# The third and the last norm of a two-block transformer kernel: sums and roots on 128 columns, widened by four small products

## The chip, the cores and the metric

The kernel runs on one core of a Trainium2 chip. The metric is the device time of one execution in microseconds. The engines are TensorE (PE; its weight loads are listed as PEld), VectorE (DVE), ScalarE (ACT), GpSimd (POOL) and SyncE (SP), which issues the DMAs. Each has its own queue of instructions and works it off in order. They wait for each other by semaphores.

## The reference, cut to what matters

Two transformer layers follow each other on x with 512 tokens of 1024 features. Each has mixers and a feed-forward, and a norm over the features stands before each. The two norms that the change touches are the ones of the second layer:

```python
def _rms(x, w):
    xf = x.astype(jnp.float32)
    y = xf * lax.rsqrt(jnp.mean(xf * xf, axis=-1, keepdims=True) + EPS)
    return (y * w.astype(jnp.float32)).astype(x.dtype)

h = _rms(x, norm1_w[l]) * (1 + sc1) + sh1        # third norm, "r3": input of the second layer
proj = h @ w_in[l]
...
x = x + g1 * (mixed @ w_out[l])
h2 = _rms(x, norm2_w[l]) * (1 + sc2) + sh2       # last norm, "r6": input of its feed-forward
x = x + g2 * _conv_ffn(h2, w_up[l], conv_w[l], conv_b[l], w_down[l])
```

sc1, sh1, g1, sc2, sh2 and g2 come from a product of the conditioning vector c with w_mod (the "modulation").

## The kernel before, in words

**Layout.** x lies in SBUF as eight tiles of 128 features by 512 tokens (P = 128, KT = 8 tiles, S = 512 tokens, NT = 4 token blocks of 128). Weights come in chunks of 128x2048: SyncE loads a chunk (`load_chunk`, L113), ScalarE rounds it to its high part (`round_chunk`, L121), VectorE makes the low part (`rest_chunk`, L127), and TensorE multiplies in three passes, high by high, high by low, low by high (`split_mm`, L133 to L135). High and low parts have two slots each, so a chunk is rounded while the one before it is multiplied.

**A norm** (class `Norm`, L167 to L207). ScalarE squares the eight tiles (L179), GpSimd adds the first of them into `acc` (L188), and TensorE adds over the features: a product of a 128x128 matrix of ones with `acc` (L194) and with each square tile that was not added (L197). The result is the sum of each token, the same in all 128 rows of a bank, for 512 tokens. ScalarE takes the root of mean plus EPS (L202), 128x512, and VectorE the reciprocal (L207), 128x512, into `root`, which other products on VectorE then use as a full tile. An fp32 product appears in the trace as two records.

**Third norm, r3.** It stands at the end of the block with the first layer's feed-forward. GpSimd adds six squares, TensorE adds the sum and the last square tile (`r3.pe_sum(pe, k, KT - 2, [KT - 1])`), and then makes six modulation reductions (L447), each of three products with one column, 36 records together. ScalarE's order at the end of this block is: last square, root, rounding of the second weight chunk of the next block. VectorE's is: last addition to x, reciprocal, low part of that chunk. Then the semaphores of the block are cleared and all engines meet at a barrier. The next block begins with eight tiles scaled by VectorE (`shifted_dve`: L227 scales, L235 makes the low part) and rounded by ScalarE (`shifted_act`, L242); TensorE multiplies each as it comes.

**Last norm, r6.** It stands between the output projection of the second layer and its feed-forward, in one block. GpSimd adds four squares, and TensorE adds their sum and four square tiles (`r6.pe_sum(pe, k, KT - 5, list(range(KT - 4, KT)))`). ScalarE's order there is: rounding of a feed-forward chunk, squares 6 and 7, root, then the eight roundings of `shifted_act`. VectorE's is: last additions to x (L2415), low part of that chunk (`rest_chunk(dve, k, (OUT2 + 5) % 2, OUT2 + 6)`), reciprocal, wait for it, `shifted_dve`. TensorE goes on with the first feed-forward chunk, tile by tile as the scaled tiles are split (`ffn2.pe_up(pe, i, h6_split if i == 0 else None)`). The two first chunks of the feed-forward are loaded, rounded and split before the reciprocal.

**Small products that the kernel already has.** `group_sums` (L646) and the lag weights (L2152) write 32 rows of a bank each, with 32 columns of weights; `group_spread` (L651) and the state inputs (L2128) read 32 rows each.

**Order.** Nothing is planned by a program: the order on each engine is the order in which its code is written out.

Of the kernel before, what the change touches and what calls it, by code (L numbers as in the profile page):

```python
# [9 lines left out]
ACT = mybir.ActivationFunctionType  # L10
# [3 lines left out]
P = 128  # L14
S = 512
D = 1024
KT = D // P
NT = S // P
# [7 lines left out]
EPS = 1e-6  # L26
# [140 lines left out]
class Norm:  # L167
# [37 lines left out]
    def dve_invert(self, dve):  # L205
        dve.wait_ge(self.rooted, 1)
        dve.reciprocal(self.root[:, :], self.root[:, :]).then_inc(self.inverted, 1)  # L207

# [388 lines left out]
def program(nc, io):  # L597
    root_ctx = ExitStack()
    with root_ctx:
        k = Core()  # L600
# [9 lines left out]
        def sb(name, shape, dt=F, ctx=root_ctx):  # L610
            return ctx.enter_context(nc.sbuf_tensor(name, shape, dt))
# [12 lines left out]
        eps_col = sb("eps_col", [P, 1])  # L624
        sqrt_first = sb("sqrt_first", [P, 2])
# [43 lines left out]
        def gone(ctx):  # L669
            ctx.close()  # L670
# [135 lines left out]
        with nc.Block() as block:  # L806
# [20 lines left out]
            @block.gpsimd  # L827
            def _(pool):
                pool.memset(k.ones[:, :], 1.0).then_inc(set_up, 1)
                pool.memset(eps_col[:, :], EPS).then_inc(set_up, 1)  # L830
                pool.memset(neg_ones[:, :], -1.0).then_inc(set_up, 1)
                pool.memset(windows[:, :, :, NCMP:32], 0.0).then_inc(set_up, 1)
                pool.memset(spread[:, :], 0.0).then_inc(set_up, 1)
# [580 lines left out]
        r2, r3 = Norm(k, "r2", square_sum, k.root, k.bank[6]), Norm(k, "r3", square_sum, k.root, k.bank[6])  # L1414
# [15 lines left out]
        with nc.Block() as block:  # L1430
# [82 lines left out]
            def _(act):  # L1513
# [44 lines left out]
                r3.act_root(act, KT, eps_col[:, 0:1])  # L1558
# [3 lines left out]
            def _(dve):  # L1562
# [49 lines left out]
                r3.dve_invert(dve)  # L1612
                ffn.dve_weights(dve, ffn.down_chunk(1, KT - 1) + 2)

            @block.tensor
            def _(pe):
# [40 lines left out]
                for c in range(modulation.AT_END, modulation.N):  # L1657
                    modulation.reduce(pe, c)
        gone(ffn_ctx)
# [648 lines left out]
        r6 = Norm(k, "r6", square_sum, k.root, k.bank[6])  # L2308
# [8 lines left out]
        with nc.Block() as block:  # L2317
# [31 lines left out]
            def _(act):  # L2349
# [34 lines left out]
                r6.act_root(act, KT, eps_col[:, 0:1])  # L2384
# [8 lines left out]
            def _(dve):  # L2393
# [52 lines left out]
                dve.wait_ge(r6.inverted, 1)  # L2446
# [10 lines left out]
            def _(pe):  # L2457
# [41 lines left out]
                r6.pe_sum(pe, k, KT - 5, list(range(KT - 4, KT)))  # L2499
                for half in range(2):  # L2500
                    for i in range(HALF * half, HALF * half + HALF):
                        ffn2.pe_up(pe, i, h6_split if i == 0 else None)
                    for j in range(KT):
                        ffn2.pe_down(pe, half, j)
# [146 lines left out]
```

## Time and profile before

| | us |
|---|---|
| median of 3 runs | 1347.76 (1345.07 to 1348.29) |
| profiled execution, its own time | 1347.27 |
| span of the profiled execution | 1345.5 |
| TensorE busy | 1261.2 (94%) |
| VectorE busy | 783.7 (58%) |
| ScalarE busy | 505.3 (38%) |
| GpSimd busy | 130.1 (10%) |
| mean granted clock of TensorE | 0.968 of 2.4 GHz |

The profiled execution's own time is 1.8 us longer than its span. A row of a timeline has the start and the length in us from the span's start, the engine, the line of the kernel, the operation, what is written from what, shapes and count, and in brackets how long the engine had been idle before and what ended that. A row of a group has the count, busy time in us and mean length of one in ns. TensorE's clock is given as a share: 1.00 is 2.4 GHz, 0.50 is 1.2 GHz.

### The profile page before, as it was taken

Reading aid. Unit: us, or ns where it says so; the run is one execution under the profiler, and the core shown is the slowest. Engines: PE = TensorE matmul, PEld = TensorE weight load, DVE = VectorE, ACT = ScalarE, POOL = GpSimd, SP = SyncE. Lnnn points to the kernel's source line nnn. Section 1 sums busy time; section 2 is a strip of 40 time slices with the busy share of each in tenths; the row PEclk is TensorE's granted clock in tenths of the full one; section 3 lists DMA queues with packets and bytes.
Section 4 is the critical chain, followed back from the end, with each engine's and each line's share of the span. In section 5 each row is a group of like instructions: output and inputs, shape, how many; then the busy total and the mean of one; then the engine's idle time right before and its main releaser. Section 6 shows DMA issues by size and latency. Waiting matters only on the chain. (4 is left out here: it accounts for less than half of the span.)

```text
span 1345.5 us, 15518 instructions
## 1 busy us (share of the span) xinstructions
PE 1261.2 (94%) x6278; PEld 985.3 (73%) x6278; DVE 783.7 (58%) x1254; ACT 505.3 (38%) x768; POOL 130.1 (10%) x124
## 2 busy tenths in 40 slices
PE   6999998779999999999999899769899999999999
PEld 5786675437788878888887686447678878888877
DVE  5656674234475695566554785866865553366532
ACT  5244445744432211222222722455344331233321
POOL 0000000001400170000011560003400000000000
PEclk9999999888999999999999879899989999999999
DMA  9311113010244445444443341010303222322222
GB/s 366 101 42 63 63 32 113 13 63 32 94 165 164 145 132 198 166 165 164 135 160 112 98 75 58 1 64 32 125 32 97 101 77 90 121 94 94 84 98 84
DMA packets 24678, 138.42 MB, mean 103 GB/s; under 512 B 2623, under 2 KB 4896, under 8 KB 15264
## 3 DMA queue, kind: packets, MB, share of 16 engines
q1 hardware_dynamic: 24608, 137.43, 30.4%
q8 instruction: 50, 0.82, 0.2%
q14 instruction: 20, 0.16, 0.0%
HBM read 133.75 MB, written 3.67 MB: 102 GB/s over the span
## 5 line engine op out<-in xcount | busy, mean ns | idle before, releaser
L133 PE MATMUL bank<-xhi_ffn,w_hi_part 128*128 128x512 f32 x704 | 278.7, 396 | 6.6 <-DVE xlo_ffn L235 6.6
L134 PE MATMUL bank<-xlo_ffn,w_hi_part 128*128 128x512 f32 x704 | 277.7, 394 | 0.0
L135 PE MATMUL bank<-xhi_ffn,w_lo_part 128*128 128x512 f32 x704 | 275.9, 392 | 0.0
L121 ACT ACTIVATE w_hi_part<-w_raw 128x2048 fp32r<-128x2048 f32 (+1 forms) x96 | 165.7, 1726 | 275.4 <-PE bank L135 270.4
L127 DVE TENSOR_TENSOR w_lo_part<-w_raw,w_hi_part 128x2048 fp32r<-128x2048 f32 (+1 forms) x96 | 198.8, 2071 | 88.9 <-ACT w_hi_part L121 85.6
L133 PEld LDWEIGHTS bank<-xhi_ffn,w_hi_part 128*128 128x128 f32 x704 | 133.3, 189 | 36.6 <-issue 7.6
L135 PEld LDWEIGHTS bank<-xhi_ffn,w_lo_part 128*128 128x128 f32 x704 | 133.2, 189 | 29.6
L134 PEld LDWEIGHTS bank<-xlo_ffn,w_hi_part 128*128 128x128 f32 x704 | 132.9, 189 | 27.9 <-issue 0.2
L362 DVE SCALAR_TENSOR_TENSOR squares<-bank,param,squares 128x511 f32<-128x511 f32 x88 | 63.9, 747 | 86.0 <-ACT squares L345 84.4
L134 PE MATMUL bank<-hlo_half,w_hi_part 128*128 128x512 f32 x240 | 96.6, 402 | 0.0
L133 PE MATMUL bank<-hhi_half,w_hi_part 128*128 128x512 f32 x240 | 96.0, 400 | 0.5 <-DVE hlo_half L334 0.5
L133 PE MATMUL bank<-hhi,w_hi_part 128*128 128x512 f32 x240 | 94.6, 394 | 1.7 <-DVE hlo L370 1.7
L135 PE MATMUL bank<-hhi_half,w_lo_part 128*128 128x512 f32 x240 | 95.3, 397 | 0.0
L134 PE MATMUL bank<-hlo,w_hi_part 128*128 128x512 f32 x240 | 93.6, 390 | 0.0
L135 PE MATMUL bank<-hhi,w_lo_part 128*128 128x512 f32 x240 | 93.5, 390 | 0.0
L437 DVE SCALAR_TENSOR_TENSOR mod_acc<-mod_w,mod_c,mod_acc 128x384 f32<-128x384 f32 x112 | 75.7, 676 | 2.6
L133 PE MATMUL bank<-xhi,w_hi_part 128*128 128x512 f32 x144 | 61.2, 425 | 11.5 <-DVE w_lo_part L937 11.5
L345 ACT ACTIVATE squares<-bank,param 128x512 f32<-128x512 f32 x44 | 31.9, 776 | 84.1 <-PE bank L135 84.1
L135 PE MATMUL bank<-xhi,w_lo_part 128*128 128x512 f32 x144 | 57.1, 397 | 0.0
L322 DVE TENSOR_TENSOR squares<-bank,rms_root 128x512 f32<-128x512 f32 x22 | 15.2, 691 | 71.6 <-PE bank L135 71.5
L134 PE MATMUL bank<-xlo,w_hi_part 128*128 128x512 f32 x144 | 56.8, 394 | 0.0
L133 PEld LDWEIGHTS bank<-hhi_half,w_hi_part 128*128 128x128 f32 x240 | 45.7, 190 | 13.9 <-issue 1.5
(365 smaller groups left out, 2024.6 us busy)
## 6 DMA issues: line engine op xcount, KB each, us to landing
mod_w<-in_w_mod SPq DMA_DIRECT2D x32, 768.0 KB, 4.4
w_raw<-in_w_gu SPq DMA_DIRECT2D x22, 1024.0 KB, 4.8
w_raw<-in_w_down SPq DMA_DIRECT2D x32, 704.0 KB, 4.1
w_raw<-in_w_up SPq DMA_DIRECT2D x22, 1024.0 KB, 4.7
w_raw<-in_w_in_f SPq DMA_DIRECT2D x9, 1024.0 KB, 5.1
w_raw<-in_w_out SPq DMA_DIRECT2D x8, 1024.0 KB, 4.8
w_raw<-in_w_in SPq DMA_DIRECT2D x5, 1024.0 KB, 4.9
x<-in_x SPq DMA_DIRECT2D x4, 512.0 KB, 8.6
```

What stands on the lines that cost most here:

```text
L121: act.activation(k.whi[:, slot, 0:width], k.raw[:, slot, 0:width], ACT.Copy).then_inc(k.w_hi, 1)
L127: dve.tensor_tensor(k.wlo[:, slot, 0:width], k.raw[:, slot, 0:width], k.whi[:, slot, 0:width].bitcast(F), ALU.subtract).then_inc(k.w_lo, 1)
L133: pe.matmul(out, whi, xhi, start=first, stop=False)
L134: pe.matmul(out, whi, xlo, start=False, stop=False)
L135: return pe.matmul(out, wlo, xhi, start=False, stop=last)
L322: dve.tensor_tensor(gate, k.bank[a][:, :], root, ALU.mult).then_inc(self.gated, 1)
L345: act.activation(k.sq[:, s, :], k.bank[s][:, :], ACT.Identity, bias=bias[:, 2 * i + a:2 * i + a + 1], scale=taps[:, 6 * i + 3 * a + 2:6 * ...
L362: dve.scalar_tensor_tensor(out=y, in0=k.bank[s][:, 0:S - back], scalar=taps[:, tap:tap + 1], in1=y, op0=ALU.mult, op1=ALU.add).then_inc(se ...
L437: ins = dve.scalar_tensor_tensor(out=acc, in0=w, scalar=self.c[:, j:j + 1], in1=acc, op0=ALU.mult, op1=ALU.add)
```

## The change

The third and the last norm become a `QuarterNorm`. Its sum makes, of each tile, four products of 128 columns (one block of tokens each) with 32 columns of ones; the product of token block q is written to rows 32q to 32q + 31 of one bank, all in columns 0 to 127. Root and reciprocal then work on 128x128. The root is taken of 1024 times mean plus EPS (a second constant column, filled by GpSimd at the start), so it is 32 times as large. Four products with 32 rows each then add 32 equal rows of the reciprocal into all 128 rows, each in the columns of its token block and in a bank of its own (banks 2 to 5). ScalarE copies two of the four results into `root`, VectorE the other two. At r3 the widening stands behind the second of the six reductions on TensorE, and the copies stand before the rounding and the low part of the next chunk; at r6 VectorE waits for all four copies before it scales.

```diff
@@ -205,6 +205,54 @@
     def dve_invert(self, dve):
         dve.wait_ge(self.rooted, 1)
         dve.reciprocal(self.root[:, :], self.root[:, :]).then_inc(self.inverted, 1)
+
+
+class QuarterNorm(Norm):
+
+
+    def __init__(self, k, name, acc, root, bank, wide):
+        super().__init__(k, name, acc, root, bank)
+        self.wide, self.small = wide, acc[:, 0:P]
+        self.widened, self.copied = k.sem(f"{name}_widened"), k.sem(f"{name}_copied")
+
+    def pe_sum(self, pe, k, added, tail):
+        pe.wait_ge(self.added, added)
+        for n, j in enumerate([None] + list(tail)):
+            if j is not None:
+                pe.wait_ge(self.squared, j + 1)
+            src = self.acc if j is None else k.sq[:, j % 4, :]
+            for q in range(NT):
+                mm = pe.matmul(self.bank[32 * q:32 * q + 32, 0:P], k.ones[:, 0:32], src[:, P * q:P * q + P],
+                               start=(n == 0), stop=(n == len(tail)))
+        mm.then_inc(self.summed, 1)
+
+    def act_root(self, act, n, eps_col):
+        act.wait_ge(self.summed, 1)
+        act.activation(self.small, self.bank[:, 0:P], ACT.Sqrt, bias=eps_col, scale=1024.0 / (P * n))\
+            .then_inc(self.rooted, 1)
+
+    def dve_invert(self, dve):
+        dve.wait_ge(self.rooted, 1)
+        dve.reciprocal(self.small, self.small).then_inc(self.inverted, 1)
+
+    def pe_widen(self, pe, k):
+        pe.wait_ge(self.inverted, 1)
+        for q in range(NT):
+            pe.matmul(self.wide[q][:, P * q:P * q + P], k.ones[32 * q:32 * q + 32, :],
+                      self.small[32 * q:32 * q + 32, :], start=True, stop=True).then_inc(self.widened, 1)
+
+    def copy(self, q):
+        return self.root[:, P * q:P * q + P], self.wide[q][:, P * q:P * q + P]
+
+    def act_copy(self, act):
+        for q in (0, 1):
+            act.wait_ge(self.widened, q + 1)
+            act.activation(*self.copy(q), ACT.Copy).then_inc(self.copied, 1)
+
+    def dve_copy(self, dve):
+        for q in (2, 3):
+            dve.wait_ge(self.widened, q + 1)
+            dve.tensor_copy(*self.copy(q)).then_inc(self.copied, 1)
 
 
 def plain_round(act, norm, hi, src, gain):
@@ -622,6 +670,7 @@
         spread = sb("spread", [P, 2 * P])
         k.ones = sb("ones", [P, P])
         eps_col = sb("eps_col", [P, 1])
+        eps_wide = sb("eps_wide", [P, 1])
         sqrt_first = sb("sqrt_first", [P, 2])
         mods = sb("mods", [P, 48])
 
@@ -827,6 +876,7 @@
             @block.gpsimd
             def _(pool):
                 pool.memset(k.ones[:, :], 1.0).then_inc(set_up, 1)
+                pool.memset(eps_wide[:, :], 1024.0 * EPS)
                 pool.memset(eps_col[:, :], EPS).then_inc(set_up, 1)
                 pool.memset(neg_ones[:, :], -1.0).then_inc(set_up, 1)
                 pool.memset(windows[:, :, :, NCMP:32], 0.0).then_inc(set_up, 1)
@@ -1411,7 +1461,8 @@
         hlo = sb("hlo_half", [P, HALF, S], R, ffn_ctx)
         ghi, glo = hhi[:, 0:KT, :], hlo[:, 0:KT, :]
         modulation = Modulation(k, io, sb, ffn_ctx, pr, mods, keep_sem)
-        r2, r3 = Norm(k, "r2", square_sum, k.root, k.bank[6]), Norm(k, "r3", square_sum, k.root, k.bank[6])
+        r2 = Norm(k, "r2", square_sum, k.root, k.bank[6])
+        r3 = QuarterNorm(k, "r3", square_sum, k.root, k.bank[6], k.bank[2:6])
         ffn = FeedForward(k, "ffn", GU, io["w_gu"], io["w_down"], xhi, xlo, hhi, hlo, following=2)
         gn_sq, gn_sq_v, gn_took, gn_root, gn_inv, gn_wide, gn_scaled, gn_hi, gn_lo, added1 = (
             k.sem(f"group_{w}") for w in ("squared", "squared_v", "taken", "rooted", "inverted", "spread", "scaled",
@@ -1555,7 +1606,8 @@
                             r3.act_square(act, k, x[:, j, :], j)
                         if half == 0 or j < KT - 1:
                             ffn.act_weights(act, ffn.down_chunk(half, j) + 2)
-                r3.act_root(act, KT, eps_col[:, 0:1])
+                r3.act_root(act, KT, eps_wide[:, 0:1])
+                r3.act_copy(act)
                 ffn.act_weights(act, ffn.down_chunk(1, KT - 1) + 2)
 
             @block.vector
@@ -1610,6 +1662,7 @@
                             dve.scalar_tensor_tensor(out=scale1, in0=scale1, scalar=1.0, in1=pr("norm1"), op0=ALU.add,
                                                      op1=ALU.mult)
                 r3.dve_invert(dve)
+                r3.dve_copy(dve)
                 ffn.dve_weights(dve, ffn.down_chunk(1, KT - 1) + 2)
 
             @block.tensor
@@ -1656,6 +1709,8 @@
                 r3.pe_sum(pe, k, KT - 2, [KT - 1])
                 for c in range(modulation.AT_END, modulation.N):
                     modulation.reduce(pe, c)
+                    if c == modulation.AT_END + 1:
+                        r3.pe_widen(pe, k)
         gone(ffn_ctx)
 
 
@@ -2305,7 +2360,7 @@
         sum_b = sb("square_sum_ssm", [P, S], ctx=tail_ctx)
         r5 = Norm(k, "r5", square_sum, root_a, k.bank[6])
         r4 = Norm(k, "r4", sum_b, root_b, k.bank[7])
-        r6 = Norm(k, "r6", square_sum, k.root, k.bank[6])
+        r6 = QuarterNorm(k, "r6", square_sum, k.root, k.bank[6], k.bank[2:6])
         h6_scaled, h6_rounded, h6_split = k.sem("norm2_scaled"), k.sem("norm2_rounded"), k.sem("norm2_split")
         out_a, part_a, part_b, added_a, added_b, stored = (
             k.sem(f"out2_{w}") for w in ("attn", "attn_scaled", "ssm_scaled", "attn_added", "added",
@@ -2381,7 +2436,8 @@
                         r6.act_square(act, k, x[:, j, :], j)
                     if c == 3:
                         round_chunk(act, k, n % 2, 16 * (n // 2 + 1), n - 1)
-                r6.act_root(act, KT, eps_col[:, 0:1])
+                r6.act_root(act, KT, eps_wide[:, 0:1])
+                r6.act_copy(act)
                 shifted_act(act, k, h6_scaled, h6_rounded, lambda j: shift2[:, j:j + 1], xhi)
                 for half in range(2):
                     for i in range(HALF * half, HALF * half + HALF):
@@ -2443,7 +2499,8 @@
                 from_ssm(3)
                 rest_chunk(dve, k, (OUT2 + 5) % 2, OUT2 + 6)
                 r6.dve_invert(dve)
-                dve.wait_ge(r6.inverted, 1)
+                r6.dve_copy(dve)
+                dve.wait_ge(r6.copied, 4)
                 shifted_dve(dve, k, h6_scaled, h6_rounded, h6_split, x, lambda j: scale2[:, j:j + 1],
                             lambda j: shift2[:, j:j + 1], xhi, xlo)
                 for half in range(2):
@@ -2497,6 +2554,7 @@
                 out2(3, bank_b[3], 0, k.w_used)
                 pe.wait_ge(part_a, 6)
                 r6.pe_sum(pe, k, KT - 5, list(range(KT - 4, KT)))
+                r6.pe_widen(pe, k)
                 for half in range(2):
                     for i in range(HALF * half, HALF * half + HALF):
                         ffn2.pe_up(pe, i, h6_split if i == 0 else None)
```

## Rows read from the trace of the kernel before

**Rows 1.** The page, part 1: busy time, share of the span, records of TensorE.
```profile
PE 1261.2 (94%) x6278; PEld 985.3 (73%) x6278; DVE 783.7 (58%) x1254; ACT 505.3 (38%) x768; POOL 130.1 (10%) x124
```

**Rows 2.** Timeline around r3: start, length, engine, line, operation, idle before.
```profile
732.56 1.13 PE L197 MATMUL bank<-squares,ones 128*128 128x512 f32 x2 [0.58 <-ACT squares L179]
733.52 4.07 PE L447 MATMUL bank<-ones,mod_acc 128*128 128x1 f32 x36
733.72 0.69 ACT L202 ACTIVATE rms_root<-bank,eps_col 128x512 f32<-128x512 f32 x1 [1.22 <-PE bank L197]
734.31 1.90 ACT L121 ACTIVATE w_hi_part<-w_raw 128x2048 fp32r<-128x2048 f32 x1
734.44 3.35 DVE L207 RECIPROCAL rms_root<-rms_root 128x512 f32<-128x512 f32 x1 [2.60 <-ACT rms_root L202]
737.71 2.23 DVE L127 TENSOR_TENSOR w_lo_part<-w_raw,w_hi_part 128x2048 fp32r<-128x2048 f32 x1
742.06 1.42 DVE L227 SCALAR_TENSOR_TENSOR squares<-x,mods,rms_root 128x512 f32<-128x512 f32 x2 [2.12 <-PEq L1663]
...
744.50 0.77 PE L133 MATMUL bank<-xhi_in,w_hi_part 128*128 128x512 f32 x1 [6.91 <-DVE xlo_in L235]
```

**Rows 3.** Timeline around r6.
```profile
968.44 1.23 ACT L179 ACTIVATE squares<-x 128x512 f32<-128x512 f32 x2
968.92 2.29 DVE L127 TENSOR_TENSOR w_lo_part<-w_raw,w_hi_part 128x2048 fp32r<-128x2048 f32 x1
...
969.12 1.98 PE L197 MATMUL bank<-squares,ones 128*128 128x512 f32 x4 [0.19 <-ACT squares L179]
...
971.14 0.69 ACT L202 ACTIVATE rms_root<-bank,eps_col 128x512 f32<-128x512 f32 x1 [1.47 <-PE bank L197]
971.86 3.35 DVE L207 RECIPROCAL rms_root<-rms_root 128x512 f32<-128x512 f32 x1 [0.66 <-ACT rms_root L202]
975.25 1.41 DVE L227 SCALAR_TENSOR_TENSOR squares<-x,mods,rms_root 128x512 f32<-128x512 f32 x2
...
977.69 0.77 PE L133 MATMUL bank<-xhi_ffn,w_hi_part 128*128 128x512 f32 x1 [6.58 <-DVE xlo_ffn L235]
```

**Rows 4.** Timelines of small products: 32 rows written (L2152), 32 rows read (L651).
```profile
834.92 2.02 PE L2152 MATMUL bank<-c_lifted,b_turned 128*32 128x128 f32 x64
...
82.68 1.14 PE L651 MATMUL bank<-head_roots,spread 32*128 32x512 f32 x8
...
298.19 2.09 PE L651 MATMUL bank<-square_sum,spread 32*128 32x512 f32 x8 [4.16 <-DVE square_sum L1568]
```

**Rows 5.** Groups by line and shape, small operations of VectorE and ScalarE.
```profile
L1054 DVE RECIPROCAL sq_cmp<-sq_cmp 128x31 f32<-128x31 f32 x1 | 0.3, 342 | 0.0
L1384 DVE SCALAR_TENSOR_TENSOR keep<-bank,soft 128x128 f32<-128x128 f32 x4 | 1.1, 284 | 0.0
...
L900 ACT ACTIVATE sq_cmp<-bank,eps_col 128x31 f32<-128x31 f32 x1 | 0.3, 286 | 2.1 <-PE bank L1244 2.1
L1358 ACT ACTIVATE attn<-bank 128x128 f32<-128x128 f32 x4 | 1.1, 282 | 0.1
```

**Rows 6.** Stretches: length, TensorE busy (records), granted clock, DMA share, GB/s.
```profile
297.80:297.90 0.10, 0.00 (x0) 0.50 0.00 0
...
738.10:738.20 0.10, 0.00 (x0) 0.50 0.00 0
748.30:748.40 0.10, 0.10 (x1) 0.80 0.00 0
...
973.60:973.70 0.10, 0.00 (x0) 0.60 1.16 492
...
983.80:983.90 0.10, 0.10 (x2) 0.70 0.00 0
```

**Rows 7.** Timeline of the first microseconds.
```profile
0.87 0.10 POOL L830 MEMSET eps_col<- 128x1 f32 x1
...
5.72 1.28 ACT L212 ACT_TABLE_LOAD   x1 [5.72 <-DMA x<-in_x]
```

## The prediction

> **What bounds the kernel now.** I read the page first: TensorE is busy for 94% of the span [rows 1], so only the stretches in which it waits, or runs at its lower clock, have anything to give. Then I read the timeline of the two norms that the change touches. In both the reader should follow one chain: the last square on ScalarE, its sum on TensorE, the root on ScalarE, the reciprocal on VectorE, and what follows the reciprocal. Last I read the granted clock around both.
>
> At r6 the chain is bare. The last pair of squares ends at 969.67 (968.44 + 1.23), the last sums end at 971.10, the root runs 971.14 to 971.83, the reciprocal 971.86 to 975.21, the first scaled tile starts at 975.25, and TensorE begins the feed-forward at 977.69 after 6.58 us without a product [rows 3]. Behind that nothing but TensorE decides, so what is cut here reaches the end of the kernel.
>
> At r3 it is not bare. The reciprocal ends at 737.79, but VectorE then makes the low part of the next weight chunk (737.71 to 739.94), then comes the end of the block, and the next stage's first scaled tile is at 742.06 [rows 2]. That low part needs the high part, which ScalarE makes from 734.31 to 736.21, directly after the root. So there the reciprocal's place is the last thing but one, and ScalarE's queue stands close behind it.
>
> The clock: it falls to half (1.2 GHz) at 973.6, inside r6's gap, and returns to 2.4 GHz at 983.8, which is 6.1 us after the first product; in r3's gap it falls at 738.1 and is back at 748.3, 3.8 us after the first product at 744.50 [rows 2, 3, 6].
>
> **The change, part by part.**
>
> *Sums.* One full product (two records of 512 columns) becomes four products of 128 columns with 32 columns of weights, eight records, each product in its own 32 rows of the bank. The nearest row is 64 records of 128 columns with 128*32 weights, in all four row blocks of a bank: 2.02 us together, 0.03 us each, where a stream of them in line would need four times that [rows 4]. So the four run beside each other. A last tile cost 1.13 us before (732.56 to 733.69) [rows 2]; now I take 0.5 us: two passes, their spread and the run-out. The other bound is no overlap, about 1.1 us, as before.
>
> The Trainium skill has a rule that speaks against this: "TensorE: Matmul & The Clock Gate", section "The mechanism", says that a weight load overlaps a running product only if the row group differs, and here all 128 rows are used each time. By that rule the eight records of a tile would stand in line and cost as much as now. The row of 64 records disagrees with it, and I go by the row.
>
> *What that is worth at r6.* Without the change the root ends at 971.83. With it the sums end near 970.2 and the root near 970.6. But VectorE is busy until 971.21 with the low part of a weight chunk [rows 3], and the reciprocal stands behind it in VectorE's order. So it starts at 971.24 instead of 971.86: 0.6 us won, not 1.6, and even sums in line would cost only 0.2 of that. This is what is late next.
>
> *Root.* 0.69 us for 512 columns [rows 3], 286 ns for 31 [rows 5]; in proportion 0.37 us for 128.
>
> *Reciprocal.* 3.35 us for 512 columns [rows 3], 0.34 us for 31 [rows 5]: 6.26 ns a column, so 0.95 us for 128. It saves 2.40 us at either place. At r6 it ends at 972.19.
>
> *Widening, new.* Four products of 32 rows, eight records, into four banks. Eight such records with 512 columns take 1.14 us at full clock and 2.09 us at half clock [rows 4, 6]. For 128 columns I take 0.1 us to start and 0.8 us (bounds 0.5, for a quarter of the columns with the run-out kept, and 1.1, the same eight records at full clock with all 512 columns). Before, the clock fell 2.5 us after the last sum [rows 3, 6]; the widening now comes 2.1 us after it, so it may meet the lower clock, and this is why I don't take the lower bound. At r6 the fourth product ends at 973.1.
>
> *Copies, new.* ScalarE and VectorE take two each. Copies of 128x128 from a bank are 282 ns on ScalarE, and an operation of VectorE on 128x128 from a bank is 284 ns [rows 5]. Two in a row, the first begun while the last products run, and the wait for all four: 0.6 us after the last product (bounds 0.4 and 0.9). Scaling would start at 973.7; I take 973.75 against 975.25.
>
> So at r6: 0.6 + 2.4 - 0.9 - 0.6 = **1.5 us earlier** (bounds 0.9 and 2.0). The first product of the feed-forward moves from 977.69 to 976.2.
>
> *Clock at r6.* During the first 6.1 us TensorE ran at half, which cost 3.1 us [rows 3, 6]. The gap that remains (970.2 to 976.2, with only the widening in it) is still long, so the clock will still fall. When it comes back is not tied to the first product alone: 6.1 us here, 3.8 us at r3. I take the middle, 5.0 us, which gives back (6.1 - 5.0)/2 = 0.6 us. Bounds: a return at the same moment as now costs half of the shift (0.75 us lost); a return after 3.8 us gives 1.2 us.
>
> *r3.* Sum 0.6 earlier (nothing is in VectorE's way there), root to 733.45, reciprocal to 734.45. But the widening stands behind two of the six reductions in TensorE's order: 36 records take 4.07 us [rows 2], 12 take 1.4, to about 734.4, so it runs 734.6 to 735.4. ScalarE's two copies end near 735.8. The rounding of the next chunk (1.90 us) stands behind them: it ends at 737.7 where it ended at 736.21. VectorE's low part (2.23 us), which waited for nothing but the reciprocal, now waits for that rounding and starts at 737.75 instead of 737.71. So 2.4 us of reciprocal buy nothing: **0.1 us later** with the wait between engines. TensorE's remaining 24 reductions end near 738.1 at full clock and near 740.8 if the clock is already down (twice 0.113 each), which is 0.9 us behind the low part and would be the upper bound. The lower bound is 0.3 us earlier. SyncE's first transfers of the next block move with its start, by the same 0.1 us; the weights of its first products are rounded in this block.
>
> *Small parts.* Six more products in r3's sums and fifteen in r6's cost nothing: the sums of the earlier tiles stand before a wait for squares (TensorE waits 0.58 us for the last one at r3 and 0.19 us at r6 [rows 2, 3]); without that cover they would be in the 1.1 us bound of a tile. Changing between full array, column blocks and row blocks: the Trainium skill ("TensorEngine Tiling (Array Packing)", "Key Properties") says that a change of mode drains the array. It gives no figure; no term of the sum takes one from it. The new constant is one more fill on GpSimd in the first microsecond (such a fill takes 0.10 us), while ScalarE waits for x until 5.72 [rows 7]: nothing, or 0.1 us without that cover. No weight transfer is issued later at r6, since SyncE waits for low parts that are made before the reciprocal. Two more semaphores to clear at the block's end: under 0.1 us.
>
> **Sum.** +0.1 - 1.5 - 0.6 = -2.0 us. Against the profiled execution, 1347.27 us (span 1345.5), that is 1345.3. The median of the three runs shown is 0.5 higher, so I forecast 1345.8 for the median. 0.3%, about 4.0 us, is what a measurement of this kernel can tell from no change; the forecast is inside it.
>
> **Rivals.**
> *The clock helps more.* The work left in the gap, or the moment at which it begins, spares the half-clock stretch of r6: 3.1 us instead of 0.6, so 1345.8 - 2.5 = 1343.3. For it: the gap shrinks and the widening stands in it. Against: at r3 the clock fell with reductions running nearly to that moment [rows 2, 6], so small products did not hold it there. Chance 0.14. In its better half, with 0.5 us more at the widening and a fast r3, it passes -4.
> *The clock takes back.* It returns at the same moment as now, or later for r3: +0.75 instead of -0.6, giving 1347.1. For it: 3.8 and 6.1 us differ without a reason in the work. Chance 0.22.
> *The change doesn't do what it says.* The small products stand in line, and widening plus copies take 2.5 us: r6 gains 3.0 - 0.2 - 2.5 = 0.3 us, giving 1347.5 with no clock gain. Against: rows 4. Chance 0.07.
> *Slower, through ScalarE's place at r3.* ScalarE waits for the widening with the next chunk's rounding queued behind it, and TensorE reaches the widening late and on a low clock. The block ends 0.9 us later by the bound above; the next stage's first product at 744.50 then comes after 745, and if the clock's return moves from 3.8 us behind it to r6's 6.1, another 1.2 us go. With r6's lower bound (0.9) and its clock at the same moment (+0.75): 0.9 + 1.2 - 0.9 + 0.75 = +1.95, or 1349.7. It decides once the block's end moves by more than r6 gains, 1.5 us. Chance 0.09.
> The forecast itself keeps 0.48.
>
> **How the numbers follow.** The forecast's own range is 1344.5 to 1347.0. The range given, 1342.9 to 1348.3, takes in the first three rivals with the 1.5 us or so by which runs of one kernel lie apart, and leaves out the slow end and the best of the clock. Faster by over 0.3% (under 1343.7) needs the first rival or a lucky median: 0.16. Slower by over 0.3% (over 1351.8) needs more than the slower rival gives: 0.04. Within: 0.80.
>
> **What would show it.** Right: last sum records at r6 ending near 970.2 relative to squares at 969.67; a reciprocal of about 0.95 us that starts when the low part ends; scaling 2.5 us after the low part's end (before 4.0); a gap before the first product of about 5 us; at r3 the rounding after two small copies and the low part waiting for ScalarE, the next stage at 742 +/- 0.5. Wrong: column-block products at 0.1 us each, copies over 0.4 us, TensorE's reductions as the last work of r3's block, or a clock that never falls in r6's gap.

## The result, and the profile after

| | before | after |
|---|---|---|
| median of six runs, us | 1345.55 (1342.59 to 1348.29) | 1358.09 (1355.93 to 1361.02) |
| profiled execution, its own time, us | 1347.27 | 1361.0 |
| its span, us | 1345.5 | 1359.1 |
| mean granted clock | 0.968 | 0.962 |

The ratio is 1.0113, with an interval of 1.0093 to 1.0133: the changed kernel is 1.1% slower (0.9% by the medians), where the prediction had it the same, at 1345.8 us. The ratios here and below are estimated from the single runs and differ from the quotient of the medians by up to 0.2%. Two executions further on, one of the kernel before (4341 us) and one of e2_noshift (5534 us), took several times as long as all others and are in no median and no ratio.

The page of after answers to [rows 1]; the second line is a group of its part 5 (line, operation, count, then busy us and mean ns of one, then idle time before it and what ended that):

```profile
PE 1279.8 (94%) x6336; PEld 989.8 (73%) x6336; DVE 779.7 (57%) x1258; ACT 506.2 (37%) x772; POOL 130.2 (10%) x125
...
L133 PE MATMUL bank<-xhi_ffn,w_hi_part 128*128 128x512 f32 x704 | 279.2, 397 | 3.1 <-DVE xlo_ffn L283 3.1
```

TensorE is busy 18.6 us longer (1279.8 for 1261.2), with only 58 records of small products added (6336 for 6278). The wait ahead of the feed-forward's first product is 3.1 us instead of 6.6, but the widening now stands in the gap and splits it: from the end of the last sum to that product it is 5.6 us (976.97 to 982.60) for 6.6 before. So the last norm's own chain is shorter, and the loss has to be looked for elsewhere.

**The last norm of after**, the timeline that answers to [rows 3]:

```profile
975.26 1.23 ACT L179 ACTIVATE squares<-x 128x512 f32<-128x512 f32 x2
975.75 2.28 DVE L127 TENSOR_TENSOR w_lo_part<-w_raw,w_hi_part 128x2048 fp32r<-128x2048 f32 x1
975.94 0.43 PE L225 MATMUL bank<-squares,ones 128*32 128x128 f32 x8 [1.97 <-ACT squares L179]
976.54 0.43 PE L225 MATMUL bank<-squares,ones 128*32 128x128 f32 x8 [0.17 <-ACT squares L179]
977.04 0.37 ACT L231 ACTIVATE square_sum<-bank,eps_wide 128x128 f32<-128x128 f32 x1 [0.55 <-PE bank L225]
977.95 0.94 DVE L236 RECIPROCAL square_sum<-square_sum 128x128 f32<-128x128 f32 x1
978.95 0.61 PE L241 MATMUL bank<-square_sum,ones 32*128 32x128 f32 x8 [1.97 <-DVE square_sum L236]
979.55 0.45 ACT L250 ACTIVATE rms_root<-bank 128x128 f32<-128x128 f32 x2 [2.15 <-PE bank L241]
979.64 0.49 DVE L255 COPY rms_root<-bank 128x128 f32<-128x128 f32 x2 [0.75 <-PE bank L241]
980.16 1.41 DVE L275 SCALAR_TENSOR_TENSOR squares<-x,mods,rms_root 128x512 f32<-128x512 f32 x2
...
982.60 0.77 PE L133 MATMUL bank<-xhi_ffn,w_hi_part 128*128 128x512 f32 x1 [3.05 <-DVE xlo_ffn L283]
```

From the start of the last squares to the scaling it is 4.90 us (975.26 to 980.16), where it was 6.81 (968.44 to 975.25), so 1.9 us less.

**The third norm of after**, which answers to [rows 2]:

```profile
736.29 0.63 ACT L179 ACTIVATE squares<-x 128x512 f32<-128x512 f32 x1 [5.23 <-DVE x L425]
736.97 0.42 PE L225 MATMUL bank<-squares,ones 128*32 128x128 f32 x8 [1.08 <-ACT squares L179]
737.33 1.50 PE L495 MATMUL bank<-ones,mod_acc 128*128 128x1 f32 x12
737.47 0.37 ACT L231 ACTIVATE square_sum<-bank,eps_wide 128x128 f32<-128x128 f32 x1 [0.55 <-PE bank L225]
737.87 0.95 DVE L236 RECIPROCAL square_sum<-square_sum 128x128 f32<-128x128 f32 x1 [1.61 <-ACT square_sum L231]
738.88 0.50 PE L241 MATMUL bank<-square_sum,ones 32*128 32x128 f32 x8
...
739.73 1.91 ACT L121 ACTIVATE w_hi_part<-w_raw 128x2048 fp32r<-128x2048 f32 x1
741.67 2.29 DVE L127 TENSOR_TENSOR w_lo_part<-w_raw,w_hi_part 128x2048 fp32r<-128x2048 f32 x1 [1.70 <-ACT w_hi_part L121]
```

The next stage's first scaling comes at 746.10, 9.81 us after the start of the last square; before it was 10.18 (731.88 to 742.06).

**Where the time went.** I compared the starts of ScalarE's weight roundings (L121), which mark every chunk of products, in both profiled executions. After is 2.1 us behind by 60 us and still at 223, 5.0 at 322 (the clock fell at other moments in between), 5.4 at the third norm, 6.8 at 966 us, and only 3.8 at 993 us, at the first rounding behind the last norm. From there it loses a little with every chunk, up to 13.2 at the last rounding. Of the last feed-forward, two roundings next to each other for each of its two sizes of chunk, before:

```profile
1036.66 1.91 ACT L121 ACTIVATE w_hi_part<-w_raw 128x2048 fp32r<-128x2048 f32 x1
1047.54 1.91 ACT L121 ACTIVATE w_hi_part<-w_raw 128x2048 fp32r<-128x2048 f32 x1
...
1124.23 1.38 ACT L121 ACTIVATE w_hi_part<-w_raw 128x1408 fp32r<-128x1408 f32 x1 [6.10 <-PE bank L135]
1131.71 1.38 ACT L121 ACTIVATE w_hi_part<-w_raw 128x1408 fp32r<-128x1408 f32 x1 [6.10 <-PE bank L135]
```

and after:

```profile
1041.78 1.91 ACT L121 ACTIVATE w_hi_part<-w_raw 128x2048 fp32r<-128x2048 f32 x1
1052.98 1.91 ACT L121 ACTIVATE w_hi_part<-w_raw 128x2048 fp32r<-128x2048 f32 x1
...
1124.00 1.38 ACT L121 ACTIVATE w_hi_part<-w_raw 128x1408 fp32r<-128x1408 f32 x1 [6.32 <-PE bank L135]
1131.71 1.38 ACT L121 ACTIVATE w_hi_part<-w_raw 128x1408 fp32r<-128x1408 f32 x1 [6.32 <-PE bank L135]
```

A chunk of 48 products takes 11.20 us in place of 10.88, one of 33 takes 7.70 or 7.71 in place of 7.48. With 22 and 16 such chunks that is 22 x 0.32 + 16 x 0.22 = 10.6 us, most of the 12.5 between the medians. The clock is not it. TensorE in the stretch from 1000 to 1300 us (length, TensorE busy and its products, granted clock, DMA share, GB/s), before:

```profile
1000.00:1300.00 300.00, 298.31 (x1315) 1.00 0.28 94
```

and after:

```profile
1000.00:1300.00 300.00, 299.34 (x1284) 1.00 0.27 90
```

Both run at 2.4 GHz throughout and TensorE hardly pauses, yet 31 products fewer fit in: 298.31/1315 = 226.9 ns from product to product before, 299.34/1284 = 233.1 after. No instruction of this stage was changed.

What was changed is where its tiles lie. `eps_wide`, the second constant column, is an SBUF tile of its own, and the addresses of the built program show what it does: everything that is laid down behind it is 32 bytes further on. The weight tiles stand in front and stay (`w_hi_part` at 49280, which is 128 modulo 256); in the last feed-forward the high and low input tiles that are streamed through them go from 88192 and 116864 (128 modulo 256, both) to 88224 and 116896, the hidden high and low tiles from 133248 and 155776 (128 both) to 133280 and 155808. I call the distance of a streamed tile from the weight tile, modulo 256, its relative place: 0 before, 32 after, in the whole last feed-forward. The first feed-forward had its high input tile at 0 and its low and hidden tiles at 96; now they are at 32 and 128. Its chunks of 48 products took 11.10 us before and take 11.10 after (435.00 to 446.10 before, 439.88 to 450.98 after), its chunks of 33 took 7.70 and take 7.67.

### The profile page after: what moved, and what is told of

The parts are those of the page before. It is cut to its first block and busy times, and to the rows that moved or that the text cites. A ratio compares the mean times of both kernels' runs of the same rounds, so it can differ in the third digit from the quotient of the medians.

```text
span 1359.1 us, 15643 instructions
## 1 busy us (share of the span) xinstructions
PE 1279.8 (94%) x6336; PEld 989.8 (73%) x6336; DVE 779.7 (57%) x1258; ACT 506.2 (37%) x772; POOL 130.2 (10%) x125
## 5 line engine op out<-in xcount | busy, mean ns | idle before, releaser
L133 PE MATMUL bank<-xhi_ffn,w_hi_part 128*128 128x512 f32 x704 | 279.2, 397 | 3.1 <-DVE xlo_ffn L283 3.1
L134 PE MATMUL bank<-xlo_ffn,w_hi_part 128*128 128x512 f32 x704 | 278.3, 395 | 0.0
L135 PE MATMUL bank<-xhi_ffn,w_lo_part 128*128 128x512 f32 x704 | 277.7, 394 | 0.0
L121 ACT ACTIVATE w_hi_part<-w_raw 128x2048 fp32r<-128x2048 f32 (+1 forms) x96 | 165.7, 1726 | 280.8 <-PE bank L135 277.1
L133 PEld LDWEIGHTS bank<-xhi_ffn,w_hi_part 128*128 128x128 f32 x704 | 132.4, 188 | 35.1 <-issue 3.6
L135 PEld LDWEIGHTS bank<-xhi_ffn,w_lo_part 128*128 128x128 f32 x704 | 132.5, 188 | 31.4
L134 PEld LDWEIGHTS bank<-xlo_ffn,w_hi_part 128*128 128x128 f32 x704 | 132.6, 188 | 31.2 <-issue 0.2
L133 PE MATMUL bank<-hhi,w_hi_part 128*128 128x512 f32 x240 | 95.8, 399 | 1.3 <-DVE hlo L418 1.3
L133 PE MATMUL bank<-hhi_half,w_hi_part 128*128 128x512 f32 x240 | 96.3, 401 | 0.5 <-DVE hlo_half L382 0.5
L134 PE MATMUL bank<-hlo_half,w_hi_part 128*128 128x512 f32 x240 | 95.8, 399 | 0.0
L135 PE MATMUL bank<-hhi_half,w_lo_part 128*128 128x512 f32 x240 | 95.6, 398 | 0.0
L134 PE MATMUL bank<-hlo,w_hi_part 128*128 128x512 f32 x240 | 94.8, 395 | 0.0
L135 PE MATMUL bank<-hhi,w_lo_part 128*128 128x512 f32 x240 | 94.8, 395 | 0.0
L133 PE MATMUL bank<-xhi,w_hi_part 128*128 128x512 f32 x144 | 61.9, 430 | 11.6 <-DVE w_lo_part L987 11.6
L134 PE MATMUL bank<-xlo,w_hi_part 128*128 128x512 f32 x144 | 57.7, 401 | 0.0
L135 PE MATMUL bank<-xhi,w_lo_part 128*128 128x512 f32 x144 | 57.6, 400 | 0.0
L133 PEld LDWEIGHTS bank<-hhi_half,w_hi_part 128*128 128x128 f32 x240 | 45.9, 191 | 13.2 <-issue 1.5
```

Of the source, the lines that this page charges most:

```text
L121: act.activation(k.whi[:, slot, 0:width], k.raw[:, slot, 0:width], ACT.Copy).then_inc(k.w_hi, 1)
L133: pe.matmul(out, whi, xhi, start=first, stop=False)
L134: pe.matmul(out, whi, xlo, start=False, stop=False)
L135: return pe.matmul(out, wlo, xhi, start=False, stop=last)
```

## The experiments

Theory P (place): the 32 bytes are the loss, since the spacing of the products hangs on the relative place (theory A in the texts written before the runs). Rivals: the new instructions or waits of the norms, or the phase of the clock behind them. Ratios are against the kernel before on the same chip. In the cuts of code, "..." stands for lines that only follow from those shown.

**The shift without the change, and the change without the shift**

```diff
 # e1_pad: the kernel before, with
+        unused = sb("unused", [P, 1])          # between eps_col and sqrt_first
 # e2_noshift: the changed kernel, with
-        eps_col = sb("eps_col", [P, 1])
-        eps_wide = sb("eps_wide", [P, 1])
+        eps_col = sb("eps_col", [P, 2])
+        eps_wide = eps_col[:, 1:2]
...
 # e3_shift64: the changed kernel, with
+        unused = sb("unused", [P, 1])          # behind eps_wide: 64 bytes in all
```

> The kernel before with one unused tile of 32 bytes a partition between eps_col and sqrt_first; no instruction is added, and the norms are the old ones. Theory A (the place in SBUF: the new constant column pushes every later tile up by 32 bytes, and products that read them are some 7 ns apart further): 1359 us or so, 12 to 15 above the kernel before, and feed-forward chunks of the second layer 11.20 us apart instead of 10.88. Theory B (small products leave TensorE slower behind them): no change, 1346, 10.88 us. Theory C (longer or differently placed instruction streams): no change either, 1346.

> The changed kernel with the second constant in a second column of eps_col, so that no tile moves. Theory A: second feed-forward chunks 10.88 us apart as before, and the gain of the last norm alone is left: 1343 to 1345, 1 to 4 under the kernel before. Theory B: slow chunks (11.20 us) from the last norm on, 1354 or more. Theory C: as the changed kernel, 1358.

> The changed kernel with one more unused tile of 32 bytes, so that the later tiles are up by 64 bytes. Theory A in the form that a start at a multiple of 64 bytes counts: 10.88 us chunks again, 1343 to 1345. Theory A in the form that only one certain place is good: 11.2 us chunks, 1358. Theories B and C: 1358.

| | median, us | before | ratio | us per chunk of 48 |
|---|---|---|---|---|
| e1_pad | 1359.34 (4 runs) | 1347.51 (28 runs) | 1.0092 [1.0070, 1.0114] | 11.20 |
| e2_noshift | 1348.14 (11) | 1347.51 | 1.0013 [0.9996, 1.0030] | 10.88 |
| e3_shift64 | 1351.29 (10) | 1347.51 | 1.0029 [1.0014, 1.0044] | 10.99 |

An unused tile of 32 bytes in the old kernel costs what the whole change costs. The stretch of e1_pad that answers to the two above:

```profile
1000.00:1300.00 300.00, 298.70 (x1279) 1.00 0.26 89
```

and that of e2_noshift, with the new norms and no shift:

```profile
1000.00:1300.00 300.00, 298.31 (x1315) 1.00 0.27 93
```

e2 has the 1315 products of before. P stands, and the norms are ruled out as the cause of the loss. e2's time is a miss all the same: I had expected 1343 to 1345, and it isn't faster than before. e3 fell between its two forecasts (1343 to 1345, or 1358): it is not simply further from the old place, the worse, since 64 bytes cost a third of what 32 do.

**One norm at a time**, both with `eps_wide` in the second column of `eps_col`:

```diff
 # e4_r6_noshift: third norm as before
-        r3 = QuarterNorm(k, "r3", square_sum, k.root, k.bank[6], k.bank[2:6])
+        r3 = Norm(k, "r3", square_sum, k.root, k.bank[6])
...
 # e5_r3_noshift: the same for the last norm, r6
...
```

> No tile moves, the last norm is the new one, the third norm is the old one. Theory A and my step for the third norm (worth nothing, 0.1 us later): as e2_noshift within 1 us, 1343 to 1345. If the third norm's change costs time through ScalarE's queue, this is faster than e2_noshift by what it costs.

> No tile moves, the third norm is the new one, the last norm the old one. From the traces (last square to the next stage's first scaled tile took 10.18 us with the old third norm and 9.80 with the new one in e2_noshift): 0.4 us faster than the kernel before, that is no difference that can be measured. If the third norm's change is what keeps e2_noshift 1.9 us over e4_r6_noshift, 1.5 to 2 us slower than the kernel before.

e4: 1346.67 (12 runs, before 1347.51), 0.9987 [0.9974, 1.0000]. e5: 1348.79 (12 runs, before 1348.30), 1.0010 [0.9997, 1.0023]. I had expected e4 at 1343 to 1345 too. The last norm alone is 0.13% faster (1.8 us by the ratio, 0.8 by the medians), with an interval that reaches down to no change; the third alone gains nothing. In e4's trace the last squares start at 966.52 and the scaling at 971.65, 5.13 us: 1.7 of the 1.9 us again, as in all four others with the new last norm (e2, e3, e8, e10: 5.12 or 5.13). The rest is the widening, which in e4 ran at half clock and took 0.81 us:

```profile
970.21 0.81 PE L241 MATMUL bank<-square_sum,ones 32*128 32x128 f32 x8 [1.98 <-DVE square_sum L236]
```

**Absolute or relative, and which tiles**

```diff
 # e6_allshift: the kernel before, all tiles from x on, weights too, 32 bytes on
+        unused = sb("unused", [P, 8])
 # e11_weights32: the same 32 bytes ahead of the weight tiles alone, and 224 behind them
+        unused = sb("unused", [P, 8])
...
+        unused_b = sb("unused_b", [P, 56])
 # e9_tail32: the kernel before, last feed-forward's low and hidden tiles 32 bytes on
+        unused_tail = sb("unused_tail", [P, 8], ctx=tail_ctx)
 # e10_after256: the changed kernel, everything behind eps_wide 256 bytes on
+        unused = sb("unused", [P, 56])
```

> The kernel before with an unused tile of 32 bytes in front of x, so that all tiles move up by 32 bytes, the weight tiles as well as the tiles that TensorE streams. If the place of the streamed tile by itself counts (absolute): as e1_pad, chunks of the second feed-forward 11.20 us apart, 1356 to 1360. If its place relative to the weights counts: 10.88 us, 1346.

> The kernel before with the two weight tiles up by 32 bytes and all tiles behind them up by 256. Relative theory: the streamed tiles are now 32 bytes behind the weights' place, chunks of the second feed-forward near 11.2 us and the time 10 us or more over the kernel before, though no streamed tile moved against 256. Absolute theory: as before, 10.88 us.

> The kernel before with an unused tile of 32 bytes in front of xlo_ffn2 only: xhi of the second feed-forward, and everything before it, stays; xlo_ffn2, hhi2 and hlo2 go up by 32 bytes. If the place counts product by product: the down chunks (33 products, both tiles moved) go from 7.48 to 7.70 us, the up chunks (48 products, one third of them reading the moved tile) from 10.88 to about 10.98, 22 x 0.1 + 16 x 0.22 = 5.7 us over the kernel before. If one badly placed tile slows everything: 10 to 11 us over it. If something in the constant or in an earlier stage is to blame: no change.

> The changed kernel, its constant tile included, with 224 more unused bytes, so that the later tiles are up by 256 bytes. Place theory with a period of 256 bytes: as e2_noshift, chunks of 10.88 us, 1346 to 1349, within 0.3% of the kernel before. If any shift costs: 1358.

| | relative place in the last feed-forward | products, 1000 to 1300 us | ns each | ratio |
|---|---|---|---|---|
| e6_allshift | 0 (absolute: all +32) | 1315 | 226.9 | 0.9964 [0.9947, 0.9980] |
| e11_weights32 | 224 (weights +32) | 1280 | 233.4 | 1.0076 [1.0053, 1.0099] |
| e9_tail32 | high 0, low and hidden 32 | 1289 | 231.7 | 1.0064 [1.0042, 1.0086] |
| e10_after256 | 0 (streamed tiles +256) | 1315 | 226.9 | 1.0010 [0.9993, 1.0028] |

The medians are 1344.43 (7 runs, before 1348.30), and 1359.10 (4), 1356.91 (4) and 1348.57 us (10) with 1347.83 before. e6 moves every tile and keeps the spacing, e11 leaves the streamed tiles at the same place modulo 256 and moves the weights, and pays in full. So it is the relative place, and e10 says that a whole 256 bytes are as good as none. The stretches of e6, e11 and e10:

```profile
1000.00:1300.00 300.00, 298.30 (x1315) 1.00 0.27 93
...
1000.00:1300.00 300.00, 298.71 (x1280) 1.00 0.27 92
...
1000.00:1300.00 300.00, 298.30 (x1315) 1.00 0.27 92
```

The chunks of 33 products are the cleanest measure, since both tiles that they stream, the hidden high and low, lie at one relative place. Over both feed-forwards and all runs they take 7.48 us at 0 (before, last feed-forward; e7, first), 7.70 at 32 (after, e1, e9), 7.55 at 64 (e3, last; e11, first), 7.70 at 96 (before, first), 7.67 at 128 (after, first), 7.73 at 160 (e3, first) and 7.70 at 224 (e11, last). Place 64 gives the same in either feed-forward, whichever of the tiles was moved to get there, and half of 256 is no good place.

e6 is 0.36% faster than before, with the same instructions and the same spacing. Its profile differs from before in where the clock falls (1.3 us up to 322, 0.8 at 920, 1.6 at the last norm); why that should come with all tiles moved I can't say. So two builds can lie 0.3% apart outside the interval of their runs, and differences of 0.1 to 0.3% (e2, e4, e5, e10) are no safer than that. The 0.6 to 0.9% of e1, e7, e9 and e11 are, and their chunk times show where they arise.

e9 missed. I expected 5.7 us over before in all and measured 0.64%, 8.6 us. With only the low tile moved in the up products (the chunks of 48), I expected a third of 0.32 us a chunk and measured 0.21 (1039.08, 1050.17, 1061.27: 11.09). The products of one such chunk show why:

```profile
1039.62 0.39 PE L133 MATMUL bank<-xhi_ffn,w_hi_part 128*128 128x512 f32 x1
1039.85 0.40 PE L134 MATMUL bank<-xlo_ffn,w_hi_part 128*128 128x512 f32 x1
1040.09 0.39 PE L135 MATMUL bank<-xhi_ffn,w_lo_part 128*128 128x512 f32 x1
1040.31 0.39 PE L133 MATMUL bank<-xhi_ffn,w_hi_part 128*128 128x512 f32 x1
1040.55 0.40 PE L134 MATMUL bank<-xlo_ffn,w_hi_part 128*128 128x512 f32 x1
1040.78 0.39 PE L135 MATMUL bank<-xhi_ffn,w_lo_part 128*128 128x512 f32 x1
```

From L133 to L134 and from L134 to L135 it is 0.23 to 0.24 us each, and only from L135 back to L133 is it 0.22: three products take 0.69 in place of 0.68, since the step into the low tile's product and the step out of it are both long. One product in three with a moved tile costs two thirds of the price (0.21 of 0.32). The prices of the tiles don't simply add, either: with the high tile at 32 and the low one at 128 (after, first feed-forward) a chunk of 48 takes 11.10 us, less than the 11.20 with both at 32. No run shows the rule for two tiles at different places.

**The other way round: the first feed-forward, placed well.** If P holds, its tiles at 96 leave time lying there.

```diff
 # e7_ffn1_place: the kernel before, low and hidden tiles of the first feed-forward to place 0
+        unused_ffn = sb("unused_ffn", [P, 40], ctx=ffn_ctx)
 # e8_r6_placed: e4 with that line, and the second mixer's low input tile to place 0
+        unused_in2 = sb("unused_in2", [P, 32], ctx=mix_ctx)
```

> The kernel before with an unused tile of 160 bytes in front of the tiles of the first feed-forward, so that xlo_ffn1, hhi_half and hlo_half start at the same place modulo 256 as the tiles of the second (they are 96 bytes behind it now, and products there are 231 to 234 ns apart instead of 227). The place theory: 22 chunks of 48 products faster by 0.2 us, 16 of 33 by 0.2 and 4 of 48 by 0.3, 8 to 9 us together, 1338. Anything else that differs between the two feed-forwards (VectorE's modulation products, their weight traffic): 1346, chunks 11.1 us apart as now.

> The new last norm alone, no shift from the constant, the first feed-forward placed as in e7_ffn1_place, and the low input tile of the second layer's input projection moved by 128 bytes. The place theory: e7's gain plus the 1.2 to 2 us of e4_r6_noshift, 1336 to 1337. Else 1345.

e7: 1338.46 (4 runs, before 1348.30), 0.9918 [0.9898, 0.9939]. The gain is 9.8 us by the medians, for 8 to 9 expected; by the roundings, e7 gets 8.4 us ahead between 322 us and the third norm (12.9 for 4.5), and so does e8. The rest is the clock's moments. Its chunks of 48 in the first feed-forward take 10.88 us (428.12 to 439.00) for 11.10. TensorE in the middle of that stage (small reductions are among the products), before:

```profile
420.00:680.00 260.00, 259.53 (x1152) 1.00 0.47 158
```

and in e7, with 17 more in the same time:

```profile
420.00:680.00 260.00, 258.98 (x1169) 1.00 0.48 160
```

e8: 1337.94 (5 runs, before 1348.30), 0.9920 [0.9907, 0.9933]. It beats both kernels, but stands level with e7 and a microsecond above what was expected of it (1336 to 1337): beside the placement, the new last norm shows nothing that can be told apart.

## Why the prediction was wrong

**The step that failed** is among the small parts: "The new constant is one more fill on GpSimd in the first microsecond [...]: nothing, or 0.1 us without that cover." The fill does cost nothing. The tile it fills costs 0.92% by e1, about 12.4 us (11.8 by the medians), because it moves every tile behind it. I had counted the instruction and not its storage, and had taken it that unchanged products keep their spacing. None of the rivals held this; the slower one looked for its loss at the third norm.

**Last norm, 1.5 us forecast, 1.9 measured (1.7 in the five others).** The chain was as described. The reciprocal starts at 977.95, as the low part of the weights ends (978.03), so only part of the cheaper sums counts. Reciprocal 0.94 us (0.95 forecast), root 0.37 (0.37), sums of a tile 0.43 (0.5), widening 0.61 (0.8), and 0.60 from its end to the scaling (0.6). The scaling comes 2.1 us after the low part's end, for 2.5 forecast and 4.0 before. The 0.8 us taken for the widening is what it costs at half clock (0.81 in e4).

**Sums beside each other.** Eight records of 128 columns took 0.43 us, as the row of 64 records had it [rows 4]; in line they would have taken about 1.1, what the same columns took in two records before. The Trainium skill, "TensorE: Matmul & The Clock Gate", section "The mechanism", lets a weight load overlap a running product only when the row group differs. By that rule the eight would stand in line; the trace does not agree, and the measurement decides.

**Clock at the last norm, 0.6 us forecast.** Two short stretches of after, which answer to [rows 6]:

```profile
979.20:979.30 0.10, 0.10 (x8) 0.57 2.92 492
986.00:986.10 0.10, 0.10 (x1) 0.80 0.00 0
```

It fell, as forecast, and came back 3.4 us behind the first product (982.60), not 5.0. That would give (6.1 - 3.4)/2 = 1.3 us, and with the 1.9 about the 3.0 by which after catches up there. But this is luck of one pair of executions, and the term fails as a forecast: it rests on the 6.1 us of before, the latest return of all seven profiles with the old last norm (2.8 us in e5 and e6, 2.9 in e7, 4.3 in e9, 5.2 in e1, 5.5 in e11). The six with the new one have 3.4 (after), 4.4 (e4), 4.7, 4.8, 4.8 and 5.2 (e3, e8, e10, e2). The means are 4.2 and 4.6, so on average the clock gives nothing back and takes 0.2 us. In all thirteen profiles it falls in this gap, so the rival in which it stays up falls too. Between the roundings at 966 and 993 us the six gain 2.2 to 3.0 us on before, and the six others with the old norm 0.2 to 1.6.

**Third norm, 0.1 us later forecast, 0.4 earlier measured, and then lost again behind it.** The low part waits for ScalarE (idle 1.70 us, ended by w_hi_part), so the 2.4 us of the shorter reciprocal buy next to nothing, as forecast. The rounding starts 2.8 us after the last square ends (736.92 to 739.73), for 3.3 forecast: widening and copies were shorter than I took them. It lies just beyond the lower bound of 0.3.

In two of the five profiles with the new third norm it is the upper bound that comes about: the clock falls as the widening begins, the reductions run at half clock and are the last work of the block. This is the course of the slower rival, at about half of its 0.9 us. In e3:

```profile
734.54 5.28 PE L495 MATMUL bank<-ones,mod_acc 128*128 128x1 f32 x24
...
736.90 2.29 DVE L127 TENSOR_TENSOR w_lo_part<-w_raw,w_hi_part 128x2048 fp32r<-128x2048 f32 x1 [1.70 <-ACT w_hi_part L121]
```

They end at 739.82, 0.6 us after the low part, and the first scaling comes 10.57 us after the last square, 0.4 later than before; e10 is alike. What the prediction did not look at is the stage behind. From the rounding before this norm (724.71 in before) to the one that starts at 920.86 there, the five take 197.6 to 201.9 us and have 51 us at half clock (58 in e10). The eight with the old norm take 193.9 to 197.1 and have 41 to 48. TensorE in this stretch (length, busy, granted clock) in before, in e4 (old third norm) and in e5 (new):

```profile
724.71:920.86 196.15, 165.46 (x1252) 0.90 0.21 56
...
723.84:918.94 195.10, 165.06 (x1252) 0.90 0.21 56
...
722.84:922.71 199.87, 171.53 (x1272) 0.87 0.21 55
```

In the mean the five are 4.0 us longer. This is one profiled execution of each build; by the medians e2, which has the new third norm, is 1.5 us over e4, which has the old one (0.26% by the ratios). So the third norm most likely costs 1.5 to 4 us through the clock behind it. Why the clock stays low for longer there no run was made to show.

**The sum.** Without the shift the time is e2's, +0.13% [-0.04, +0.30] against before. That is "within 0.3%", but the prediction's -2.0 us (-0.15%) lies outside it, so the sum failed in a second place as well. e4 and e5 split it into -0.13% [-0.26, 0] and +0.10% [-0.03, +0.23]. The last norm's part fits the 2.1 us forecast for it (1.5 and 0.6) but can't be told from nothing. The step that doesn't fit is the third norm's "0.1 us later", which left out the half clock behind it.

**The 13.6 us between the two profiled spans**, by the roundings: 5.0 up to 322 us, then -0.6 in the first feed-forward, 1.5 from the third norm to 920 us, 0.9 in the second layer's output projection, -3.0 at the last norm and 9.8 in the last feed-forward (10.6 by its chunks; the first of them run in part at half clock). e1, with the shift alone, has the same -0.6, 0.9 and 9.8. Of the 5.0 at the start little is the spacing: by 60 us, where products are 233 ns apart for 227 too, after is 2.1 us behind, but some 200 products make that 1.3 at most (estimate), and e2, where no tile moved, is 0.7 behind at 60 us as well. The rest was not followed to its rows; the moments of the clock before 322 us are the likely place.

## What to carry to other kernels

Before a new tile of any size goes in, look at what is laid down behind it, and compare the addresses of streamed and stationary tiles in both built programs; put a small constant in a spare column of a tile that is there, or behind all others. If products of an unchanged stage are spaced differently in two traces at the same granted clock, look for a moved tile before looking for a wait. And the same look is worth making at a kernel that nobody has changed: 160 unused bytes ahead of the first feed-forward's tiles took 0.8% off this one. A term for the clock that rests on one profile is worth little: here its moment of return behind one and the same gap moved by 3.3 us between builds.

## What was not expected of the hardware

- fp32r products of 128x512 behind each other at 2.4 GHz are 226 to 227 ns apart when the streamed tiles lie a multiple of 256 bytes from the weights (before, e2, e6, e10), 233 to 234 at 32 bytes off (either side: after and e1, and e11 at 224), 229 at 64 (e3), 232 at 128 and 234 at 160 (first feed-forward of after and e3, from their chunks of 33), and 231 to 233 where low and hidden tiles lie 96 off (before, first feed-forward). What in the chip makes it so no run here shows. The Trainium skill, "SBUF — State Buffer", section "Operand start alignment", gives the element's size as the only condition on the address and says that this is "about legality, not speed". On the speed of TensorE it says nothing, and the runs here do.
- One badly placed tile, read by every third product, stretches the step before its product as well as the one behind it: two thirds of the price (e9).
- The moment at which the clock returns after the gap at the last norm differs between builds with the same work there: 2.8 (e5, e6) to 6.1 us (before) behind the first product with the old norm, 3.4 (after) to 5.2 us (e2) with the new one.
